# Two output projections begun before the last attention units' values, and two sums of three normalisations multiplied in rounded parts

## The reference

```python
for l in range(2):
    xl = post_norm(xl, 0.5 * g1 * swiglu(modulate(xl, sh1, sc1), ffn1_w_in[l], ffn1_w_out[l]))
    hl = modulate(xl, sh2, sc2)
    # l == 0: yl = concat([gla, mla]) @ w_out        (mla: 4 heads, latent attention)
    # l == 1: yl = neighbourhood_attention(...) @ w_out   (16 heads)
    xl = post_norm(xl, g2 * yl)
    xl = post_norm(xl, 0.5 * g3 * swiglu(modulate(xl, sh3, sc3), ffn2_w_in[l], ffn2_w_out[l]))

def post_norm(x, y):
    return layer_norm(ALPHA * x + y)          # mean and variance over the 1024 features
def swiglu(h, w_in, w_out):
    gate, up = jnp.split(h @ w_in, 2, axis=-1)
    return (jax.nn.silu(gate) * up) @ w_out
```

## Time and profile before

| | us |
|---|---|
| median of three runs | 2288.67 |
| the profiled execution | 2286.92 |
| its span, first to last instruction | 2285.1 |
| PE busy | 2211.9 (97%) |
| DVE busy | 1397.5 (61%) |
| ACT busy | 972.5 (43%) |
| POOL busy | 675.8 (30%) |

### The profile page before, as it was taken

How to read it: one execution, slowest core, us unless ns; L and a number is a source line. 1 busy time by engine, 2 the same in 40 slices (tenths; PEclk the granted TensorE clock), 3 DMA queues, 4 the chain that set the end, 5 groups by cost and what they waited for, 6 DMA issues and landing times. The chain is left out here.

```text
span 2285.1 us, 33973 instructions
## 1 busy us (share of the span) xinstructions
PE 2211.9 (97%) x13172; PEld 1903.5 (83%) x13172; DVE 1397.5 (61%) x2117; ACT 972.5 (43%) x1571; POOL 675.8 (30%) x320
## 2 busy tenths in 40 slices
PE   8999999999999999999999999999999999989997
PEld 7989899988888877766788888878888878879997
DVE  4654554468887566766776766577656474346335
ACT  5665555543222255455532223253222254465443
POOL 3434245422222223321122222312222233213443
PEclk9999999999999999989999999999999999999999
DMA  8446545455454321210243543334544262214553
GB/s 283 150 166 228 216 161 195 161 194 183 176 216 184 104 96 58 83 38 19 111 147 138 194 157 107 106 139 154 186 184 161 98 147 93 75 48 156 177 181 104
DMA packets 79406, 329.98 MB, mean 144 GB/s; under 512 B 18912, under 2 KB 29280, under 8 KB 55696
## 3 DMA queue, kind: packets, MB, share of 16 engines
q1 hardware_dynamic: 79248, 327.81, 40.9%
HBM read 326.70 MB, written 1.08 MB: 143 GB/s over the span
## 5 line engine op out<-in xcount | busy, mean ns | idle before, releaser
L2209 POOL TENSOR_TENSOR WL<-WF,WH 128x1024 fp32r<-128x1024 f32 (+2 forms) x248 | 586.4, 2365 | 1388.9 <-ACT WH L1046 1388.4
L527 PE MATMUL ps<-Hh,WH 128*128 128x256 f32 (+1 forms) x2536 | 858.3, 338 | 23.4 <-DVE WL L1566 8.7
L529 PE MATMUL ps<-Hh,WL 128*128 128x256 f32 (+1 forms) x2536 | 852.9, 336 | 0.0
L528 PE MATMUL ps<-Hl,WH 128*128 128x256 f32 (+1 forms) x2536 | 852.9, 336 | 0.0
L1046 ACT CAST WH<-WF 128x1024 fp32r<-128x1024 f32 (+3 forms) x506 | 465.6, 957 | 312.0 <-PE ps L529 301.6
L527 PEld LDWEIGHTS ps<-Hh,WH 128*128 128x128 f32 x2536 | 482.5, 190 | 85.5 <-issue 28.7
L529 PEld LDWEIGHTS ps<-Hh,WL 128*128 128x128 f32 x2536 | 482.7, 190 | 50.0
L528 PEld LDWEIGHTS ps<-Hl,WH 128*128 128x128 f32 x2536 | 482.8, 190 | 49.0 <-issue 0.2
L1642 DVE CUSTOM_DVE_ANT_0 TMP<-AR 128x1024 f32<-128x1024 f32 x216 | 399.0, 1886 | 10.6 <-DMA AR<-in_ada 9.6
L1566 DVE TENSOR_TENSOR WL<-WF,WH 128x1024 fp32r<-128x1024 f32 (+2 forms) x259 | 311.9, 1205 | 121.7 <-ACT WH L1046 120.7
L527 PE MATMUL ps<-HIDh,WH 128*128 128x512 f32 (+1 forms) x880 | 307.0, 349 | 3.7 <-DVE WL L1566 3.7
(11 more groups left out here) (231 smaller groups left out, 2012.3 us busy)
## 6 DMA issues: line engine op xcount, KB each, us to landing
WF<-in_w SPq DMA_DIRECT2D x170, 1024.0 KB, 4.8
AR<-in_ada SPq DMA_DIRECT2D x120, 512.0 KB, 5.7
WF<-in_w SPq DMA_DIRECT2D x80, 704.0 KB, 4.1
AR<-in_piece SPq DMA_DIRECT2D x12, 1024.0 KB, 8.3
AR<-bias_rows SPq DMA_DIRECT2D x3, 1024.0 KB, 13.1
AR<-in_rpb SPq DMA_DIRECT2D x12, 256.0 KB, 6.6
AR<-in_cond SPq DMA_DIRECT2D x2, 1024.0 KB, 6.9
X<-in_x SPq DMA_DIRECT2D x2, 512.0 KB, 4.3
```

Of the source, the lines that this page charges most:

```text
L527: e.matmul(out, lh, rh, start=first, stop=False, skip_group_check=parts)
L528: e.matmul(out, lh, rl, start=False, stop=False, skip_group_check=parts)
L529: return e.matmul(out, ll, rh, start=False, stop=end, skip_group_check=parts)
L2209: e.tensor_tensor(l[:, k0:k1, :], src[:, k0:k1, :], h[:, k0:k1, :].bitcast(F32), ALU.subtract).then_inc(*up("p_lo", ("lo", i, 1)))
```

## The change

1. `pe_attention` gets `leave=2` for "mla": the values of the last two units, 14 and 15, are not weighted in its loop but by `rest()`, which `pe_lin` calls after two rows of eout's first chunk. That chunk takes its rows in the order 0, 1, 2, 4, 5, 6, 7, 3, and signals ("half", i) only at its end.
2. `pe_attention_pairs` gets `steps=1` for "na": the transposes of unit 31 and the values of units 30 and 31 are done by `rest()` after row 3 of nout's first chunk.
3. In the normalisations after f10, f20 and f11, `SUM` and `SQ` are split into a rounded high part (ACT, into Hh 6 and 7) and a low part (DVE, into Hl 6 and 7); PE multiplies each in two fp32r matmuls with a rounded copy `avg_r` of `avg`, instead of one fp32 matmul.
4. The exponential of the root is made in two halves of 256 columns, latents first, and tile 0 waits for its own half. The multiplication of tile 1 by the root is made for the latents ahead of tile 0's low part and for the context behind it. This holds for mix0, f20, f11 and mix1; f21 has only latents.

```diff
@@ -258,6 +258,7 @@
     VEC = sb("VEC", VN)
     SC = sb("SC", KT * 32)[:, :].rearrange("p (k c) -> p k c", k=KT)
     MOD = sb("MOD", 2 * 72 * 2)[:, :].rearrange("p (l n r) -> p l n r", l=2, r=2)
+    avg_r = sb("AVG", P, F32R)[:, :]
     with nc.sbuf_tensor("LAT", [P, 8 * 512], F32R) as LAT_:
         pass
     ROW = sb("ROW", 512)[:, :]
@@ -386,6 +387,10 @@
     AFTER = {"f10": CH["e_lr"][0], "mix0": CH["f20_gu"][1], "f20": CH["f11_gu"][1], "f11": CH["n_q"][0], "mix1": CH["f21_gu"][1],
              "f21": None}
 
+
+
+    ROUNDED = ("f10", "f20", "f11")
+
     def slot_freed(i, q):
 
         n = TURN[i]
@@ -528,7 +533,8 @@
         e.matmul(out, lh, rl, start=False, stop=False, skip_group_check=parts)
         return e.matmul(out, ll, rh, start=False, stop=end, skip_group_check=parts)
 
-    def pe_lin(e, i, of, T, tiles, fresh=False, mid=None, wide=2):
+    def pe_lin(e, i, of, T, tiles, fresh=False, mid=None, wide=2, order=None):
+
 
 
         h, l = parts_of(i)
@@ -537,25 +543,27 @@
         for c0 in range(0, len(tiles), wide):
             group = tiles[c0:c0 + wide]
             out = [ps.take(e, t, *freed) for t, freed in group]
-            for k in range(n):
+            for x, k in enumerate(order or range(n)):
                 hi, lo, ready = of[k]
                 if c0 == 0 and k in (0, kc):
                     e.wait_ge(*at(("hi", i, int(k >= kc))))
                     e.wait_ge(*at(("lo", i, int(k >= kc))))
                 if c0 == 0 and fresh:
-                    for x in ready:
-                        e.wait_ge(*at(x))
+                    for y in ready:
+                        e.wait_ge(*at(y))
                 for c, (t, _) in enumerate(group):
                     col = slice(P * (c0 + c), P * (c0 + c) + P)
-                    m = pe_product(e, out[c][:, 0:T], h[:, k, col], l[:, k, col], hi[:, 0:T], lo[:, 0:T], k == 0, k == n - 1)
-                    if k == n - 1:
+                    m = pe_product(e, out[c][:, 0:T], h[:, k, col], l[:, k, col], hi[:, 0:T], lo[:, 0:T], x == 0, x == n - 1)
+                    if x == n - 1:
                         over = c0 + c == len(tiles) - 1
                         m.then_inc(*up("tile", ("done", t), *([("end", i)] if over else []),
-                                       *([("half", i)] if over and len(tiles) > wide else [])))
-                    elif len(tiles) <= wide and k == kc - 1 and c == len(group) - 1:
+                                       *([("half", i)] if over and (order or len(tiles) > wide) else [])))
+                    elif not order and len(tiles) <= wide and k == kc - 1 and c == len(group) - 1:
                         m.then_inc(*up("half", ("half", i)))
                         if mid:
                             mid()
+                if order and x == 1:
+                    mid()
 
     def pe_pair(e, of, *chunks):
 
@@ -744,9 +752,9 @@
                 if n == len(blocks) - 1:
                     m.then_inc(*up("weigh", (name, "weigh", i + x)))
 
-    def pe_attention_pairs(e, name, units, work, do):
+    def pe_attention_pairs(e, name, units, work, do, steps=3):
         n = len(units)
-        for i in range(n + 3):
+        for i in range(n + steps):
             if i < n and i % 2 == 0:
                 pe_scores_pair(e, name, i, units)
             for item in work[i]:
@@ -761,7 +769,7 @@
                         pe_pieces(e, "y")
                     pe_stat(e, ("y", end // 4), S, [(HT[10], ("ysum", end // 4)), (HT[11 + end % 2], ("ysq", end))])
 
-    def pe_attention(e, name, units, work, do):
+    def pe_attention(e, name, units, work, do, leave=0):
         n = len(units)
         for i in range(n + 3):
             if i < n:
@@ -770,7 +778,7 @@
                 do(e, *item)
             if 0 <= i - 2 < n:
                 pe_turn(e, name, i - 2, units[i - 2])
-            if 0 <= i - 3 < n:
+            if 0 <= i - 3 < n - leave:
                 pe_weigh(e, name, i - 3, units[i - 3])
 
     def pe_work1(e, what, j):
@@ -815,10 +823,19 @@
     def pe_means(e, st, T):
         s1 = ps.take(e, (st, "m1"), (st, "mu"))
         s2 = ps.take(e, (st, "m2"), (st, "var"))
-        e.wait_ge(*at((st, "sum", 6)))
-        e.matmul(s1[:, 0:T], avg, SUM[:, 0:T], start=True, stop=False)
-        e.wait_ge(*at((st, "sq", 6)))
-        e.matmul(s2[:, 0:T], avg, SQ[:, 0:T], start=True, stop=False).then_inc(*up("stat", (st, "sumread")))
+        if st in ROUNDED:
+            e.wait_ge(*at(("avg",)))
+            e.wait_ge(*at((st, "suml")))
+            e.matmul(s1, avg_r, Hh[:, 6, :], start=True, stop=False)
+            e.matmul(s1, avg_r, Hl[:, 6, :], start=False, stop=False)
+            e.wait_ge(*at((st, "sql")))
+            e.matmul(s2, avg_r, Hh[:, 7, :], start=True, stop=False)
+            e.matmul(s2, avg_r, Hl[:, 7, :], start=False, stop=False)
+        else:
+            e.wait_ge(*at((st, "sum", 6)))
+            e.matmul(s1[:, 0:T], avg, SUM[:, 0:T], start=True, stop=False)
+            e.wait_ge(*at((st, "sq", 6)))
+            e.matmul(s2[:, 0:T], avg, SQ[:, 0:T], start=True, stop=False)
         e.wait_ge(*at((st, "x", 7)))
         e.matmul(s1[:, 0:T], avg, X[:, 7, 0:T], start=False, stop=True).then_inc(*up("stat", (st, "m1")))
         e.wait_ge(*at((st, "xsq", 7)))
@@ -963,11 +980,18 @@
             pe_product(e, b, hi[:, c], lo[:, c], h[:, 0, T2:2 * T2], l[:, 0, T2:2 * T2], True, True).then_inc(
                 *up("tile", ("done", ("mv", t)), *([("end", i), ("half", i)] if t == 3 else [])))
         some(1)
-        pe_attention(e, "mla", units3, work3, pe_gla)
+        pe_attention(e, "mla", units3, work3, pe_gla, 2)
+
+        def rest():
+
+            for i in (14, 15):
+                pe_weigh(e, "mla", i, units3[i])
+
         ae = [(*hf[h], [("mll", h, 1)]) for h in range(4)] + [(*hf[4 + h], [("gol", h)]) for h in range(4)]
         for c in range(4):
             pe_lin(e, CH["eout"][c], ae, T2, [(("mix0", "d", j), [("mix0", "x", j)]) for j in (2 * c, 2 * c + 1)], fresh=c == 0,
-                   mid=(lambda: pe_shift(e, "mix0", T2)) if c == 2 else None, wide=1 if c == 3 else 2)
+                   mid={0: rest, 2: lambda: pe_shift(e, "mix0", T2)}.get(c), wide=1 if c == 3 else 2,
+                   order=None if c else (0, 1, 2, 4, 5, 6, 7, 3))
         pe_means(e, "mix0", T2)
 
     def pe_na_work(e, what, i):
@@ -983,11 +1007,17 @@
         pe_pair(e, acts(hf, "mix1h", "mix1l"), (CH["n_k"][0], T2, [(("nk", j), [("nk", j)]) for j in range(2)]),
                 (CH["n_q"][0], S, [(("nq", j), [("nq", j)]) for j in range(2)]))
         pe_na_work(e, "nv", 0)
-        pe_attention_pairs(e, "na", units4, work4, pe_na_work)
+        pe_attention_pairs(e, "na", units4, work4, pe_na_work, 1)
+
+        def rest():
+
+            pe_turn(e, "na", 31, units4[31])
+            pe_weigh_pair(e, "na", 30, units4)
+
         an = [(*hu[k], [("nol", k)]) for k in range(KT)]
         for c in range(4):
             pe_lin(e, CH["nout"][c], an, S, [(("mix1", "d", j), [("mix1", "x", j)]) for j in (2 * c, 2 * c + 1)], fresh=c == 0,
-                   mid=(lambda: pe_shift(e, "mix1", S)) if c == 2 else None, wide=1 if c == 3 else 2)
+                   mid={0: rest, 2: lambda: pe_shift(e, "mix1", S)}.get(c), wide=1 if c == 3 else 2)
         pe_means(e, "mix1", S)
 
     def pe_program(e):
@@ -1241,7 +1271,10 @@
         e.wait_ge(*at((st, "var")))
         e.activation(r, t, ACT.Ln, bias=cst("eps_post")).then_inc(*up("ln", (st, "ln")))
         e.wait_ge(*at((st, "ln")))
-        e.activation(r, r, ACT.Exp, scale=-0.5).then_inc(*up("root", (st, "root")))
+        for h in range(T // S):
+            c = slice(S * h, S * h + S)
+            e.activation(r[:, c], r[:, c], ACT.Exp, scale=-0.5).then_inc(
+                *up("root", (st, "root", h), *([(st, "root")] if h == T // S - 1 else [])))
 
     def act_modulate(e, st, before, l, g, T):
         e.wait_ge(*at(("mod", l, g)))
@@ -1250,7 +1283,7 @@
             for r in range(T // S):
                 c = slice(S * r, S * r + S)
                 up_, sh = MOD[:, l, 8 * (g + 1) + k, r:r + 1], MOD[:, l, 8 * g + k, r:r + 1]
-                e.wait_ge(*at((st, "res", k) if k else (st, "mt", r)))
+                e.wait_ge(*at((st, "res", k) if k > 1 else (st, "res", 1, r) if k else (st, "mt", r)))
                 if k:
                     if k >= 3:
                         e.wait_ge(*at((st + "l", k - 3)))
@@ -1290,6 +1323,11 @@
                 if h:
                     for k in {4: (0, 1), 5: (2, 3), 6: (4, 5, 6)}.get(n, ()):
                         act_collect(e, st, k, T)
+            if h and st in ROUNDED:
+                e.wait_ge(*at((st, "sum", 6)))
+                e.copy(Hh[:, 6, :], SUM).then_inc(*up("h_hi", (st, "sumh")))
+                e.wait_ge(*at((st, "sq", 6)))
+                e.copy(Hh[:, 7, :], SQ).then_inc(*up("h_hi", (st, "sqh")))
         act_last(e, st, T)
 
     def act_roots(e, *norms):
@@ -1497,6 +1535,7 @@
```

(14 more changed lines are left out.)

## The result

| | median us | runs | range | to before |
|---|---|---|---|---|
| before, beside the changed kernel | 2288.51 | 8 | 2285.73 to 2292.78 | |
| changed | 2282.80 | 8 | 2281.58 to 2284.52 | 0.9977 [0.9968, 0.9985] |
| changed, a second series | 2285.00 | 11 | 2281.49 to 2287.06 | 0.9987 [0.9979, 0.9996] |

The first series is 5.7 us (0.25%) faster where 2.6 was forecast, the second 3.2. Both are within 0.3%, and both medians are inside the range. The two series of the same kernel differ by 2.2 us, nearly as much as the whole forecast, so the medians alone don't confirm its size. The part that the code earned can be read from the traces, in stretches with an equal granted clock, to about a tenth of a microsecond.

What follows compares the result with a forecast made beforehand. TensorE (PE), busy 97% of the span, was taken as the bound. Terms -1.95 (mla), +1.35 (na), -1.03 (sums) and -0.94 (halves) gave -2.6 us, so a median of 2286.1 us, range 2282 to 2291.

Steps and rivals of the forecast that it cites:

- Bound: Whole kernel: PE busy 97% of the span; only its own work or places where it stands can move the time.
- 1, mla: End of mla attention: twelve eout matmuls fill PE's hole, then row 4 waits 0.75 for a low half; -1.95 us.
- 2, na: End of na attention: the 0.88 wait stays and nout[1] waits 1.3 us for its late low half; +1.35 us.
- 3, sums: Norms after f10, f20, f11: rounded sums shorten PE's work; -0.53, -0.25, -0.25, together -1.03 us.
- 4, halves: Before mix0, f20, f11, mix1: PE starts 0.47 earlier, kept only in f20 and f11; -0.94 us.
- Sum: Whole kernel: the four terms -1.95, +1.35, -1.03 and -0.94 give -2.6 us.
- The shared access: Norms after f10, f20, f11: VectorE's unbroken run keeps GpSimd out, new subtractions undelayed, about 0.7 us each.
- the first rival: Norms after f10, f20, f11: GpSimd gets in ahead of the new subtractions; sums cost +3.6, total +2.0 us; 12%.
- Median: Whole kernel: forecast median 2286.1 us, 0.11% faster, against 2288.7 before.

Runs made afterwards that it cites:

- na_split_early: Changed kernel with ScalarE and VectorE splitting nout's second chunk before the last value's cast, TensorE's order kept: 2283.32 us, 0.9979 to before.
- only_na: Kernel before with only the na reordering and the cast of avg: 2290.07 us, 1.0009 to before.
- na_fixed: Changed kernel with unit 31's transposes ahead of nout's 24 matmuls and nout[1] split before the last value's cast: 2281.58 us, 0.9970; again 2282.63, 0.9979.
- lows_first: Changed kernel with VectorE's two new subtractions ahead of its weight split instead of behind it: 2291.14 us, 1.0013 to before.

## Why the prediction was right, point by point

- **Bound.** Held: every gain and loss sits at a place where PE stands or works less.
- **1, mla, forecast -1.95, measured -1.87 and alone -1.89.** The mechanism and its wait for the low half are as told (0.57 and 0.34 idle instead of 0.75 and 0.3).
- **2, na, forecast +1.35, measured +1.99.** The step was right: nout[1] starts 1.32 us later. What I missed comes behind it. I wrote that all that follows hangs on PE and moves along. It doesn't: at 2047.81 GpSimd gets in ahead of VectorE, whose addition into SUM (L1901) takes 1.72 us and not 0.42 as the same one (L1856) did. GpSimd's second instruction then starts at 2050.26, again ahead of VectorE, whose next low half (issued at 2050.50, the first of the x2 below) takes 3.43 us instead of 1.22. So VectorE has no idleness left before L1869 (0.73 before), and the last input of the norm's sums comes later: PE's wait for x 7 is 0.79 and was 0.38. That is 0.18 more up to the sums and 0.49 behind them. That na_split_early is back at before's time shows that all of it descends from the late split. The single links are read from traces, not tested: both profiles of the changed kernel and only_na have the 1.72 and the 3.43, na_split_early and na_fixed have 0.42 and 1.22.

```profile
2047.81 2.49 POOL L2257 TENSOR_TENSOR WL<-WF,WH 128x1024 fp32r<-128x1024 f32 x1 [31.55 <-ACT WH L1076]
2047.96 0.87 DVE L1892 SCALAR_TENSOR_TENSOR X<-ps,MOD,X 128x256 f32<-128x256 f32 x2
...
2048.86 1.72 DVE L1901 TENSOR_TENSOR SUM<-X 128x256 f32<-128x256 f32 x1
...
2050.50 4.57 DVE L1605 TENSOR_TENSOR WL<-WF,WH 128x1024 fp32r<-128x1024 f32 x2
...
2067.97 0.70 PE L840 MATMUL ps<-X,CST 128*128 128x256 f32 x2 [0.79 <-DVE X L1892]
```

- **3, sums, forecast -0.53 -0.25 -0.25, measured alone -0.48 -0.40 -0.41.** After f20 I let ScalarE's split of weights bind as in the earlier trace rows. It does: the variance is released by the square on ScalarE. But the square begins 2.68 us after the sums (before 2.77), and the semaphore behind it costs 0.03 and not 0.08, so the variance starts 3.30 after the sums instead of the 3.45 I had, and 3.70 before. The bound was the right one, its size was misread. In the earlier trace rows the square at 1488.41 starts 0.03 after the end of L823 (1487.36 and 1.02), as the split ends: it waited for PE's sum too. In the changed kernel it waits for nothing and starts 0.10 before the end of the split in front of it:

```profile
1482.90 1.03 ACT L1076 CAST WH<-WF 128x1024 fp32r<-128x1024 f32 x1
1483.84 0.59 ACT L1269 ACTIVATE TMP<-ps 128x512 f32<-128x512 f32 x1
```

- **4, halves, forecast 0 -0.47 -0.47 0, measured alone -0.27 -0.47 -0.48 -0.30.** The 0.47 at the start is exact. For the mixers I had found 0.2 us of slack at the second row and wrote that the delay eats it, so that nothing is left. That is the wrong way round: the tile's low part is ready at the same moment as before, 0.2 us before PE took it, so PE may be 0.2 earlier, and is. In the whole kernel, with part 3 ahead, the four places gave -0.73, -0.47, -0.87, -0.70, in sum -2.77 against -1.97.
- **Sum.** -1.87 + 1.99 - 2.77 = -2.65; the table has -2.55 with 0.10 of drift in stages that the change does not touch. The errors +0.08, +0.64 and -0.80 cancel.
- **The shared access.** GpSimd did not get ahead of the new subtractions; in lows_first it did, with the price of the first rival. In both, an unbroken run of VectorE keeps it out, and a gap of 0.09 us is enough to let it in. Once in, it holds the access for its whole instruction: in both cases it ends 2.26 us after VectorE's last instruction (1480.71 to 1482.97, and 1484.53 to 1486.79). The Trainium skill ("SBUF — State Buffer", section "Who interferes with whom") says this of VectorE's two-port modes, "for the whole instruction", and the trace agrees. That issue order decides who blocks, as the section says, doesn't agree with the trace: VectorE's L1605 at 1478.29 and, in lows_first, L1884 at 1483.84 were issued after GpSimd's instruction and passed it undelayed.
- **Median.** 2286.1 was forecast, 3.3 over the first series and 1.1 over the second. The traces show -2.55. In the first series a part of the rest goes with the granted clock: its mean over the 8 runs was 0.9926, that of before about 0.991 in the other series (beside this one it is not on record), worth 2.4 us by the slope. What the second series has beyond the traces, at an equal clock, is under 1 us and stays unexplained; it may be scatter.

## What to carry to other kernels

Moving matmuls into a hole pays only if what the hole waited for is still ahead of them: here twelve matmuls gained 1.9 us, and twenty-four that came before the transposes gained nothing and made the engine behind them late by their own length (the values start 6.04 us after the transposes behind the idle 1.82, before 3.12). When work is put ahead of a chain, ask what hangs behind that chain on the other engines and how much slack each has; here 1.60 us of the 2.92 were covered and 1.32 were not, and another 0.67 were lost behind them. On a shared access, keep the short instructions that matter in one unbroken run: the order that puts them behind ready work was 1.4 us per norm better than the one that puts them first and lets them wait 0.09.

## What the runs showed of the hardware

- A two-input subtraction of 512 columns on VectorE took 0.69 us or 2.71 us by whether it followed the instruction before it without a gap or after one of 0.09 us, with GpSimd waiting.
- Two rounded (fp32r) passes of 512 columns cost 0.23 us each where a fp32 matmul cost 0.86.
- The kernel before's executions in one series differ by 9 us (2283.99 to 2293.05), with the mean granted clock between 0.988 and 0.993. In the profiles the clock fell behind idleness of PE (3.48 us at the start, 3.08 in mla, 1.82 in na) in some executions and, behind the same idleness, not in others. That filling a hole with unused matmuls leaves the median where it was is shown for one hole, the one in mla.
